# One weight of 40 columns for the sample tokens' high and low parts in the input projection of a hybrid decoder step

## The reference, cut to what matters

```
h = rmsnorm(x, ln1)
p = h @ w_in                       # 3352 columns
q, kv, gt, rq, rk, rv, rg = split(p)
q, k = rope(q, pos), rope(k, pos)  # also rq, rk
gates = sigmoid(gt)
```

## Time and profile before

| | |
|---|---|
| median of 3 runs | 2100.44 us |
| lowest and highest | 2099.89 and 2104.41 us |
| profiled execution | 2098.01 us |
| its span, first to last instruction | 2096.2 us |
| mean granted clock of TensorE | 0.974 of full |
| TensorE busy | 1943.9 us, 93% |
| VectorE busy | 1047.5 us, 50% |
| ScalarE busy | 744.9 us, 36% |
| GpSimd busy | 711.1 us, 34% |
| projection, stage 1 | to 316 us of the span |
| projection, stage 2 | 316 to 460 us of the span |

### The profile page before, as it was taken

One profiled execution on the slowest core, in us unless ns is written; L12 is line 12 of the kernel. 1 busy time (PEld: TensorE's weight loads), 2 busy tenths in 40 slices (PEclk: granted clock), 3 DMA queues, 4 the chain that ended last, 5 costly groups with the idle time before them and its releaser, 6 DMA issues. The chain is left out here.

```text
span 2096.2 us, 33992 instructions
## 1 busy us (share of the span) xinstructions
PE 1943.9 (93%) x12757; PEld 1678.8 (80%) x12757; DVE 1047.5 (50%) x1809; ACT 744.9 (36%) x1497; POOL 711.1 (34%) x724
## 2 busy tenths in 40 slices
PE   6999999977999999968999989799999999999996
PEld 4777767855777777747777868599999999999996
DVE  5634433553434444366777863454443453433546
ACT  4301101201233333336777863342223322233232
POOL 0111111220322222144455652263444434345450
PEclk9999999988999999979999999899999999999998
DMA  6121101137688776353000022112122111221123
GB/s 185 33 100 41 41 3 67 67 114 141 102 113 112 97 98 91 51 86 81 11 18 24 2 71 91 62 41 61 41 61 61 41 41 41 61 62 41 41 91 122
DMA packets 156964, 141.99 MB, mean 68 GB/s; under 512 B 16569, under 2 KB 138122, under 8 KB 156482
## 3 DMA queue, kind: packets, MB, share of 16 engines
q1 hardware_dynamic: 152706, 131.43, 27.4%
q0 software_dynamic: 4096, 8.40, 2.6%
HBM read 124.27 MB, written 19.69 MB: 69 GB/s over the span
## 5 line engine op out<-in xcount | busy, mean ns | idle before, releaser
L2071 PE MATMUL banks<-halves 128*128 128x258 f32 (+2 forms) x5760 | 703.7, 284 | 16.2 <-DVE core L2320 10.0
L2071 PEld LDWEIGHTS banks<-halves 128*128 128x128 f32 x5760 | 698.2, 190 | 20.5 <-issue 13.9
L444 POOL TENSOR_TENSOR halves<-core,halves 128x512 fp32r<-128x512 f32 (+3 forms) x239 | 355.4, 1496 | 459.1 <-ACT halves L440 459.0
L435 PE MATMUL banks<-hidden 128*128 128x512 f32 (+3 forms) x1512 | 349.7, 387 | 9.3 <-DVE hidden L444 9.2
L435 PEld LDWEIGHTS banks<-hidden 128*128 128x128 f32 (+1 forms) x1512 | 254.5, 179 | 77.9 <-issue 9.9
L440 ACT ACTIVATE halves<-core 128x512 fp32r<-128x512 f32 (+2 forms) x253 | 173.2, 700 | 385.5 <-PE banks L2071 333.4
L1128 PE MATMUL banks<-arena,blocks 128*128 128x254 f32 (+1 forms) x1152 | 247.9, 372 | 9.3 <-ACT arena L1262 5.2
L1128 PEld LDWEIGHTS banks<-arena,blocks 128*128 128x128 f32 x1152 | 209.2, 194 | 34.6 <-issue 6.1
L1696 POOL TENSOR_SCALAR arena<-arena,kept 128x64 f32<-128x64 f32 (+8 forms) x192 | 123.1, 653 | 127.6 <-DVE arena L1748 125.6
L1026 POOL DMA_DIRECT2D arena<-in_cache_kv x128 | 67.8, 530 | 233.3 <-PE banks L1172 205.4
L2332 DVE TENSOR_TENSOR core<-banks,core 128x516 f32<-128x516 f32 x144 | 99.2, 693 | 81.2 <-PE banks L2071 81.2
(11 more groups left out here) (228 smaller groups left out, 2158.8 us busy)
## 6 DMA issues: line engine op xcount, KB each, us to landing
core<-in_cache_kv SPq DMA_DIRECT2D x128, 128.0 KB, 5.3
core<-in_w_gate SPq DMA_DIRECT2D x22, 512.0 KB, 4.0
core<-in_w_up SPq DMA_DIRECT2D x22, 512.0 KB, 5.3
core<-in_w_down SPq DMA_DIRECT2D x22, 512.0 KB, 4.2
core<-in_x_prompt SPq DMA_DIRECT2D x16, 512.0 KB, 3.3
arena<-in_cache_kv SPq DMA_DIRECT2D x128, 64.0 KB, 5.9
arena<-in_cache_kv POOLq DMA_DIRECT2D x128, 64.0 KB, 4.8
retention<-in_w_in SPq DMA_DIRECT2D x16, 448.0 KB, 6.1
```

Of the source, the lines that this page charges most:

```text
L435: done = pe.matmul(out, left[a], right[b], start=(first and i == 0), stop=(last and i == 2))
L444: return engine.tensor_tensor(lo, x, hi.bitcast(F32), ALU.subtract)
L2071: done = pe.matmul(out, w[a], x[b], start=(first and n == 0), stop=(last and n == 2), skip_group_check=True)
```

## The change

The sample tokens get an array of their own, `m.hs`: per k-block 40 columns, of which 0 to 31 hold the 8 high parts four times over and 32 to 39 the 8 low parts. `m.hT` shrinks to the 1024 prompt tokens. In tile 8, TensorE issues two products per k-block: the 40 columns by the weights' high part into rows 0 to 39 of the bank, and the first 8 columns by the weights' low part into rows 0 to 7. So rows 0 to 7 hold high by high and high by low, and rows 32 to 39 low by high. VectorE, after the next chunk's low parts and before it waits for `raw_done`, waits for the products' end, copies rows 32 to 39 to `m.t2` and adds them to rows 0 to 7 in PSUM. A new semaphore, `sample_sum`, orders the two and is awaited by ScalarE before its copies of tile 8. Rows 8 to 31 are computed and not used.

```
--- before.py
+++ after.py
@@ -199,9 +199,10 @@
 
 def place_hidden(nc, ctx, m):
 
-    halves = ctx.enter_context(nc.sbuf_tensor("hidden", [P, 16 * TOK + 16 * 512], F32R))
+    halves = ctx.enter_context(nc.sbuf_tensor("hidden", [P, 16 * SEQ + 16 * 512 + 8 * 40], F32R))
     room = Room(halves, 0)
-    m.hT = [room(8 * TOK).rearrange("p (k t) -> p k t", k=8) for _ in range(2)]
+    m.hs = room(8 * 40).rearrange("p (k t) -> p k t", k=8)
+    m.hT = [room(8 * SEQ).rearrange("p (k t) -> p k t", k=8) for _ in range(2)]
     m.wk = [[room(512) for _ in range(2)] for _ in range(KT)]
     m.xt, m.sq = m.slot[0:2], m.slot[2]
     m.raw = [m.pool[:, 3584 + 512 * i:4096 + 512 * i] for i in range(NRAW)]
@@ -448,7 +449,7 @@
 PROJECT_ONLY = ("x_in0", "x_in1", "ident_in", "aw_in", "aw_hi", "aw_lo", "turned", "hT_hi", "hT_lo", "h_done", "rms_done",
                 "raw_done", "roped", "tkept", "tturned", "cos_done", "proj_done", "vkept", "w_used", "att_done",
                 "att_masked", "kd_done", "o_done", "state_done", "state_out", "gates_kept", "gates_late", "gate_done",
-                "turned_out", "rows_out") + tuple(f"slot_out{k}" for k in range(5))
+                "turned_out", "rows_out", "sample_sum") + tuple(f"slot_out{k}" for k in range(5))
 
 
 def stage_project(nc, s, m, io, first, end):
@@ -464,6 +465,9 @@
     def turned_half(i, half):
 
         b = m.banks[:, 0, :].rearrange("p (k t) -> p k t", k=4)[:, :, 0:rows(i)]
+        if i == TP:
+            v = m.hs[:, 4 * half:4 * half + 4, :]
+            return b, [v[:, :, 0:32].rearrange("p k (r t) -> p k r t", r=4), v[:, :, 32:40]]
         return b, [v[:, 4 * half:4 * half + 4, i * P:i * P + rows(i)] for v in m.hT]
 
     def staged(ch, k):
@@ -573,6 +577,8 @@
                 for half in range(2):
                     act.wait_ge(s["turned"], 2 * i + half + 1)
                     b, (hi, _) = turned_half(i, half)
+                    if i == TP:
+                        b = b.unsqueeze(2).broadcast_to(hi.shape)
                     round_to_hi(act, hi, b).then_inc(s["hT_hi"], 1)
 
             def weights_hi(ch, k):
@@ -612,6 +618,8 @@
                     wait(act, "o_done", ret_before(k + 1))
                     wait(act, f"slot_out{n % NRAW}", 16 * stored_before(n))
                 act.wait_ge(s["proj_done"], n + 1)
+                if t == TP:
+                    act.wait_ge(s["sample_sum"], 2 * ch + 2)
                 if kind == "win":
                     act.activation(m.gates[0:r, t, :], src[0:r, 256:280], ACT.Sigmoid).then_inc(s["gate_done"], 1)
                     act.activation(slot[0:r, 0:256], src[0:r, 0:256], ACT.Copy).then_inc(s["raw_done"], 1)
@@ -665,7 +673,7 @@
                 for half in range(2):
                     dve.wait_ge(s["hT_hi"], 2 * i + half + 1)
                     b, (hi, lo) = turned_half(i, half)
-                    rest_to_lo(dve, lo, b, hi).then_inc(s["hT_lo"], 1)
+                    rest_to_lo(dve, lo, b, hi[:, :, 0, :] if i == TP else hi).then_inc(s["hT_lo"], 1)
 
             def weights_lo(ch, k):
                 dve.wait_ge(s["aw_hi"], KT * ch + k + 1)
@@ -695,6 +703,12 @@
                     if t == NT - 1 and ch + 1 < end:
                         for k in range(KT):
                             weights_lo(ch + 1, k)
+                    if t == TP:
+                        part, whole = m.t2[n % 2][0:r, 0:WIDTH[ch]], m.banks[:, 6 + n % 2, 0:WIDTH[ch]]
+                        dve.wait_ge(s["proj_done"], n + 1)
+                        dve.tensor_copy(part, whole[32:32 + r, :]).then_inc(s["sample_sum"], 1)
+                        dve.wait_ge(s["sample_sum"], 2 * ch + 1)
+                        dve.tensor_tensor(whole[0:r, :], whole[0:r, :], part, ALU.add).then_inc(s["sample_sum"], 1)
 
                     slot = m.raw[n % NRAW][0:r, :]
                     x, y = heads(kind, slot), heads(kind, m.t2[n % 2][0:r, :])
@@ -794,9 +808,14 @@
                             turn_half(n + 1, TURN_STEPS.index(k))
                         if t == 0:
                             pe.wait_ge(s["aw_lo"], KT * ch + k + 1)
-                        last_mm = split_products(pe, m.banks[0:r, 6 + n % 2, 0:WIDTH[ch]],
-                                                 [x[:, k, t * P:t * P + r] for x in m.hT],
-                                                 [w[:, 0:WIDTH[ch]] for w in m.wk[k]], k == 0, k == KT - 1)
+                        out, w = m.banks[:, 6 + n % 2, 0:WIDTH[ch]], [w[:, 0:WIDTH[ch]] for w in m.wk[k]]
+                        if t == TP:
+                            pe.matmul(out[0:40, :], m.hs[:, k, :], w[0], start=(k == 0), stop=False, skip_group_check=True)
+                            last_mm = pe.matmul(out[0:r, :], m.hs[:, k, 0:r], w[1], start=False, stop=(k == KT - 1),
+                                                skip_group_check=True)
+                        else:
+                            last_mm = split_products(pe, out[0:r, :], [x[:, k, t * P:t * P + r] for x in m.hT], w,
+                                                     k == 0, k == KT - 1)
                         if t == NT - 1 and ch + 1 < end and k < KT - 1:
                             last_mm.then_inc(s["w_used"], 1)
                     last_mm.then_inc(s["proj_done"], 1)
```

## The result

The changed kernel takes 2092.1 us (median of 7 runs, 2087.79 to 2095.85) against 2101.29 for the kernel before in 7 runs beside it: a ratio of 0.995 (95% interval 0.9937 to 0.9962), some 9 to 10.5 us less. 2092.1 lies in the range, 0.9 from the forecast. The sum behind it does not hold so well: some of its terms fell short, and a gain that was in no term made up for them.

The account below looks back on a forecast made before the run. TensorE, busy 1943.9 of 2096.2 us, was taken as the bound. Terms of 5.4 + 0.7 + 0.3 + 0.6 + 0.4 = 7.4 us, against a median of 2100.44, gave 2093.0 us; range 2089.5 to 2098.0.

Parts of the forecast that it names:

- What bounds, and the products: Sample tiles: TensorE bounds; eight products fewer per chunk save 1.88 us in six chunks, 1.05 in `win`, 12.3 in all.
- The term of VectorE's sum: Each chunk's sample tile: VectorE's copy and add make the raw copy 1.43 us later, 0.94 in `win`.
- Retention: Boundaries after chunks 0, 1, 2: slack for the state gone, stall about 0.1, gain 1.8 each, 5.4 us together.
- the second form of the forecast: Retention boundaries: longer sum, rotation or waits stall each 0.5 to 1 us; total gain 3 to 6; chance 0.16.
- three times: Retention boundaries after chunks 0, 1, 2: the gain of 1.8 us taken for each, giving 5.4.
- End of stage 1: After chunk 3: TensorE's wait for line 749 ends 0.7 us earlier, carried through states, store and barrier; gain 0.7.
- That the drain could run at half clock: End of stage 1: longer TensorE idling might cost clock in the drain, within the range's microsecond of spread.
- `kv` to `win`: Turn of tile 8's keys after the next chunk's first tile: waits 1.5 us for the rotation; gain 0.3.
- `win` to `q`: Boundary before `q`: 1.05 us off the products, but the first product waits for VectorE's low weights; gain 0.6.
- end of `q`: End of stage 2: the chain goes through raw copy, rotation and line 730; 1.88 - 1.43, gain 0.4 us.
- The alternating width: Sample tile: switching 40 and 8 columns costs 0.12 us per product, so slower, 2105.7 us; chance 0.14.
- More than forecast: VectorE's sum short (0.41 us per instruction), first low weights early: retention 5.6, ends 1 more each; gain 9 to 10; chance 0.07.

Follow-up runs that it names:

- experiment 1: Kernel before with arrays moved up, ratio 0.9986; kernel before with 4096 bytes between k-blocks, 0.9978; the change without that distance, 2094.59 us, 0.9965.
- Experiment 3: The changed kernel with VectorE's copy and sum after the fourth of the next chunk's eight low parts instead of the eighth: 2089.47 us, ratio 0.9948.
- experiment 5: The changed kernel with the copy of rows 32 to 39 done twice: 2101.91 us, ratio 0.9998 to the kernel before.
- experiment 2: Kernel before with the hidden state's k-blocks 4160 bytes apart: 2101.73 us, ratio 0.9996; with 4224 bytes: 2099.85 us in a single execution.
- Experiments 3 and 4: The fourth: on Experiment 3's kernel, VectorE evacuates before rotating the sample tile, 2085.25 us; then TensorE also turns `kv`'s sample tile one step later, 2083.4 us.
- experiment 6: The changed kernel with the sample tile's two products per block on float32 operands in place of float32r: 2171.07 us, a single execution.

## Why the prediction was right and where it was not

**What bounds, and the products: right.** TensorE was the bound, the pitch follows the moving columns, and six tiles lost 1.8 each and `win` 1.0. (The prediction counts six sample tiles outside a stage's last one; they are five, and no sum uses the six.) The term of VectorE's sum (1.43 with the wait) was right: 1.40 here (97.17 to 98.57), and 1.43 more wait at the end of `q`.

**Retention: right twice, wrong once.** I worked the slack out for chunk 1, found it zero within 0.1 and a gain of 1.8, and multiplied by three. Chunks 1 and 2 gave 1.84 with waits of 0.1 (without the new distance, experiment 1, 1.83). In chunk 0 VectorE starts its low parts 1 us later, so the slack that I called zero was below zero: there the second form of the forecast held, with a stall of 0.95. The step that failed is "three times": the row of each boundary had to be read, and chunk 0's has a table load ahead of it that chunk 1's has not, in the trace of the kernel before too. The stall also took 1.6 us of clock; a rival with a stall of 0.5 to 1 us had no such term. Experiment 3 takes the stall away and the clock stays full; experiment 5 lengthens it and twice the time is spent at half. The three boundaries gave 3.0 us, not 5.4.

**End of stage 1: the sign of the first part was wrong.** TensorE's wait grew by 1.1, where 1.88 - 0.7 = 1.2 was forecast. The states' part thus ended 0.76 earlier (8.76 us behind the sample tile's start for 9.52), as forecast. That the drain could run at half clock I had named, as within the spread, and took as nothing: it made the 0.7 gained into 0.6 lost, and 1.1 came back in stage 2's first two tiles, most of it by the clock again. How much of this is the change's doing stays open: the kernel before can have the same long half level, with its short wait (experiment 2, 4160 bytes), and two more traces with the change's order there show 0.3 to 0.5 lost in place of the 0.5 gained.

**`kv` to `win`: a mis-sized term.** The mechanism was right (the turn of tile 8's keys waits for the chain). The wait was forecast at 1.5 and is 2.31. Half a microsecond is VectorE's low parts: I had them paced by ScalarE and ended at 4.96 behind the tile's start, but for 280 columns they run back to back at 0.37 each behind the evacuation and end at 5.47. The rest is in the handovers, each 0.04 to 0.12 where I had counted a part. So -0.5 for 0.3. Experiments 3 and 4 took the wait down to 0.97, 0.68 and 0.35 by moving exactly that chain.

**`win` to `q`, end of `q`: right**, 0.6 and 0.3 for 0.6 and 0.4 (0.1 to 0.2 of the 0.6 is the faster prompt tiles); the first product of `q` waits 0.3 for its weights, forecast 0.4.

**Missed altogether: the layout.** I read the smaller `m.hT` as an effect of the new array and gave it no term. Experiment 1 shows that the layout, 4096 bytes between the k-blocks of a weight, is worth 3 to 4 us here. Without it the terms sum to 3.9 in the profiled pair, not 7.4; worked on as in the prediction that makes 2096.5, inside the range but 3.5 above the forecast. The medians are kinder to the sum than the traces: the change without the distance is 7.4 us under the kernel before, by its interval 4.4 to 10.3, but its own trace has 2.7 in the projection. That the total came out 0.9 from the forecast is therefore in part luck: two misses, the terms too high and the layout left out, cancelled. How large each was, between the traces' and the medians' figures, stays open.

**The rivals.** The alternating width did not happen: 0.23 from each product to the next. The Trainium skill, TensorEngine Tiling (Array Packing), Key Properties, has a change of tiling mode drain TensorE; for this type and these widths the trace does not agree, and for float32 (experiment 6) there is a cost of 0.09 us for each change, in the rule's direction. The row on the sample tile of the kernel before, with which I weighed it, was the right one, and line 1208's 0.12 was for the most part the type and not its waits. "More than forecast" was named for a short sum; the gain over the kernel beside it, 9.2 us, reached its size, but by another way.

## What to carry to other kernels

Where the slack at a repeated boundary comes out near zero, work it out for the first one by its own rows, since start-up work (here a table load) sits there. On an engine that runs at its pitch, a stall of under a microsecond can cost more in clock than in waiting, so a chain that others wait for goes ahead of long jobs on its engine, as the early sum did here. And when a change alters an array's shape, count the distance between its blocks among the things changed.

## What was not expected of the hardware

- The layout of the weights changes the pitch of products whose weights are 128 columns wide, by the distance between k-blocks (or by that between the high and the low array, which moves with it): 5.56 to 5.58 us for 24 products at 4096 bytes, 5.65 to 5.66 at 4128, 4160 and 4224. With 280 moving columns a tile took 3.16 and 3.17 us, no difference to speak of.
- The granted clock fell to half for 3.4 us behind stalls of 0.95 us (chunk 0, after), 0.85 (the change without the distance) and 0.72 (chunk 1, copy done twice), and for 6.8 behind one of 1.66; behind 3.02 after `kv` there it fell again; behind 0.72 in chunk 2 of that same kernel, and behind 2.31 after `kv` in the change (2.30 in the change without the distance), it did not. A stall makes it likely here, not certain. At the end of stage 1 the half level lasted 17.1 us in three of nine traces with a wait of 1.2 to 1.3 us, and in five of five with 2.3 to 3.0.
- A change of the weight's width, 40 to 8 columns and back, costs float32 products 0.09 us, and the projection's float32r products nothing.
